# Expert u rows: one load of 1 MB per block, with one semaphore per buffer, in place of two half-row loads

## The reference, cut to what matters

```python
def block(xb):                                   # per block of tokens
    q = (xb @ peer_wq).reshape(PEER_BLOCK, PEER_HEADS, 2, PEER_HALF)
    s = jnp.einsum('thpd,pkd->thpk', q, peer_subkeys).astype(jnp.float32)
    ...                                          # two top-16 lists, their top-16 pairs: eidx, gate
    act = jax.nn.gelu(jnp.einsum('thkd,td->thk', peer_u[eidx], xb))
    return jnp.einsum('thk,thkd->td', gate * act, peer_v[eidx])
```

## Time and profile before

| what | value |
|---|---|
| median of 3 runs | 4359.24 us (4354.56 to 4363.43) |
| the profiled execution | 4361.14 us, its span 4359.4 us |
| TensorE (PE) busy | 4170.0 us, 96% of the span |
| DVE / ACT / POOL busy | 58% / 31% / 16% |
| column phase (blocks 0 to 127) | from about 1840 us to 3233 us |
| value phase | from about 3233 us to 4310 us |

### The profile page before, as it was taken

How to read it: one execution, slowest core, us unless ns; L and a number is a source line. 1 busy time by engine, 2 the same in 40 slices (tenths; PEclk the granted TensorE clock), 3 DMA queues, 4 the chain that set the end, 5 groups by cost and what they waited for, 6 DMA issues and landing times.

```text
span 4359.4 us, 70474 instructions
## 1 busy us (share of the span) xinstructions
PE 4170.0 (96%) x26539; PEld 4004.9 (92%) x26539; DVE 2535.9 (58%) x4045; ACT 1345.8 (31%) x1865; POOL 717.2 (16%) x513
## 2 busy tenths in 40 slices
PE   8998979989899989999999999999999999999996
PEld 6788979989587979999999999999999999999996
DVE  3323233341212355666477746666679888998986
ACT  3432211231212132232355522222223333333333
POOL 0000010020000020024200011111123333344430
PEclk9989989989968999999999999999999999999998
DMA  6532222223431212233334489999999999999993
GB/s 225 203 99 64 73 65 78 69 65 117 167 142 49 73 54 77 79 115 123 124 127 166 169 304 354 355 351 355 356 325 399 410 401 403 392 399 398 400 392 134
DMA packets 495259, 943.14 MB, mean 216 GB/s; under 512 B 126340, under 2 KB 375872, under 8 KB 443000
## 3 DMA queue, kind: packets, MB, share of 16 engines
q1 hardware_dynamic: 443520, 567.36, 39.0%
q0 software_dynamic: 51616, 374.19, 21.4%
HBM read 866.63 MB, written 73.56 MB: 216 GB/s over the span
## 4 chain that ended last, share of the span: by engine, by line
PE 92%; DVE 3%; DMA 2%; ACT 2%; DVEq 1%; issue 0%; POOL 0%; SPq 0%; ACTq 0%
PE pl L1072 24%; PE pp L196 24%; PE pp L1131 12%; PE pt L1131 6%; PE pl L1131 6%; PE pp L1040 5%; PE pt L1049 2%; PE pp L775 2%; PE pp L991 2%; PE pp L956 1%; PE pp L975 1%; PE pt L775 1%; PE pp L842 1%; PE pl L775 1%; PE pt L948 1%; PE pl L1003 1%
## 5 line engine op out<-in xcount | busy, mean ns | idle before, releaser
L1072 PE MATMUL pl<-h_hi,ut_hi 128*128 128x384 f32 x2048 | 734.7, 359 | 0.6 <-ACT ijt L1384 0.6
L1072 PE MATMUL pl<-h_hi,ut_lo 128*128 128x384 f32 x2048 | 692.3, 338 | 0.0
L1072 PE MATMUL pl<-h_lo,ut_hi 128*128 128x384 f32 x2048 | 691.3, 338 | 0.0
L1704 DVE TENSOR_TENSOR ut_lo<-pp,ut_hi 128x512 fp32r<-128x512 f32 x508 | 350.2, 690 | 483.4 <-ACT ut_hi L1337 480.8
L1337 ACT ACTIVATE ut_hi<-pp 128x512 fp32r<-128x512 f32 x508 | 304.0, 599 | 822.0 <-PE pp L1040 765.6
L211 DVE TENSOR_TENSOR w_lo<-raw,w_hi 128x2048 fp32r<-128x2048 f32 x120 | 274.7, 2290 | 425.1 <-ACT w_hi L206 425.0
L1409 ACT ACTIVATE v_hi<-v_raw 128x1024 fp32r<-128x1024 f32 x256 | 272.0, 1062 | 686.0 <-PE pl L1131 508.1
L1072 PEld LDWEIGHTS pl<-h_lo,ut_hi 128*128 128x128 f32 x2048 | 387.1, 189 | 0.0
L1072 PEld LDWEIGHTS pl<-h_hi,ut_hi 128*128 128x128 f32 x2048 | 386.2, 189 | 0.8 <-ACT ijt L1384 0.8
L1806 DVE TENSOR_TENSOR v_lo<-v_raw,v_hi 128x1024 fp32r<-128x1024 f32 x256 | 313.7, 1226 | 124.9 <-ACT v_hi L1409 121.8
L1072 PEld LDWEIGHTS pl<-h_hi,ut_lo 128*128 128x128 f32 x2048 | 384.7, 188 | 0.0
(11 more groups left out here) (359 smaller groups left out, 8262.8 us busy)
## 6 DMA issues: line engine op xcount, KB each, us to landing
u_raw<-in_peer_u SPq DMA_DIRECT2D x256, 512.0 KB
v_raw<-in_peer_v SPq DMA_DIRECT2D x256, 512.0 KB
p_f<-p_scr SPq DMA_DIRECT2D x256, 192.0 KB
raw<-in_w_in SPq DMA_DIRECT2D x24, 1024.0 KB, 5.6
g_scr<-gs POOLq DMA_DIRECT2D x6, 4096.0 KB, 13.7
raw<-in_w_mk SPq DMA_DIRECT2D x16, 1024.0 KB, 4.9
raw<-in_w_mv SPq DMA_DIRECT2D x16, 1024.0 KB, 4.8
raw<-in_w_out SPq DMA_DIRECT2D x16, 1024.0 KB, 5.8
```

The lines of the kernel that those rows point to most:

```text
L1072: last = mm(pl[:, d, 0:N], w[:, d, k, :], x[:, k, S:S + N], start=(k == 0 and w is ut_hi and x is h_hi), stop=(k == KC - 1 and w is ut_lo))
L1704: tt(ut_lo[:, d, 4 * g:4 * g + 4, :], src.rearrange("p (c i) -> p c i", c=4), ut_hi[:, d, 4 * g:4 * g + 4, :].bitcast(F32), ALU.subtract). ...
```

## The change

The two half-row loads of a block become one load of the whole rows. The four semaphores `u_in[d][h]` become two, `u_in[d]`. TensorE waits once per block, at group 0. The load waits for all four groups of block b (`t_done`), where the first half waited for two. In the steady body it stands where the first half stood, ahead of the two `p_scr` stores.

```diff
-        u_in = [[sem(f"u_in{s}{h}") for h in range(2)] for s in range(2)]
+        u_in = [sem(f"u_in{s}") for s in range(2)]
...
-            def u_load(i, d, h, free=None):
+            def u_load(i, d, free=None):
                 if free is not None:
                     sp.wait_ge(t_done, free)
-                sp.dma_start(u_raw[:, d, h * HD:(h + 1) * HD], uv[i * 2 + d][:, h * HD:(h + 1) * HD])\
-                    .then_inc(u_in[d][h], 16)
-            def next_u(i, d, h):
-                u_load(i + 1, d, h, i * 8 + (4 * d + 2 * (h + 1)))
+                sp.dma_start(u_raw[:, d, :], uv[i * 2 + d]).then_inc(u_in[d], 16)
+            def next_u(i, d):
+                u_load(i + 1, d, i * 8 + (4 * d + 4))
...
             def ahead_body(i, d):
-                for h in range(2):
-                    next_u(i, d, h)
+                next_u(i, d)
                 s_store(i + (d - 1), 1 - d)
...
             def steady_body(i, d, first=False):
                 b = i * 2 + d if isinstance(i, int) else None
                 if b is None or b + 2 < NK:
-                    next_u(i, d, 0)
+                    next_u(i, d)
...
                     p_store(i - 1, d)
-                if b is None or b + 2 < NK:
-                    next_u(i, d, 1)
                 g_load(i, d)
...
             def turn_rows(i, d, g, dst, first=False):
-                if g % 2 == 0:
-                    pe.wait_ge(u_in[d][g // 2], i * 16 + 16)
+                if g == 0:
+                    pe.wait_ge(u_in[d], i * 16 + 16)
```

More of the change, by code:

```diff
@@ L664, in _ @@
                 sp.wait_ge(lo_ready, NPANEL - 1 + d)
-                for h in range(2):
-                    u_load(0, d, h)
+                u_load(0, d)
             for d in range(2):
-                for h in range(2):
-                    next_u(0, d, h)
+                next_u(0, d)
                 if d == 1:
```

## The result

| kernel | median us | runs | ratio to before, 95% interval |
|---|---|---|---|
| before | 4359.73 (4354.56 to 4363.43) | 4 | |
| after | 4406.85 (4397.19 to 4410.68) | 4 | 1.0106 [1.0086, 1.0125] |

The change makes the kernel 47 us slower, 1.1%. The prediction was 4359 us, no change, with a range of 4351 to 4374 us; it is wrong. What came is its rival A.

What follows compares the result with a forecast made beforehand. TensorE was taken to pace the column phase, its second half beside nearly full DMA engines. Three parts of 0 each on the profiled 4361.14 us, given as the median: 4359 us, no change (83%), range 4351 to 4374 us.

Steps and rivals of the forecast that it cites:

- rival A: SP's steady body outlasts a column because sa's store lands late behind the full load: 31 us slower, 4390 us; chance 12%.
- Part 1: Removing 128 load issues on SP and 128 TensorE waits before group 2: taken as 0, at most 1.3 us faster.
- rival B: Loads of u_raw: one exposed fixed cost saved per block, up to 384 us; what remains is 3 us; chance 5%.
- Part 2: The u_raw load starts later and is needed earlier by TensorE: taken as 0, upper end 12 us, one time.
- cover of 12.7 us: Time from issuing the full load to group 0 of block b+2 reading it, 5 quarter columns later.
- one late load: In the steady part, seven gathers back to back after the gates' last store could delay a load by 12 us, once.
- Part 3: SP's reordered queue puts sa's store behind the full load; landing taken as T + 7.5 us, so the slip is 0.
- T: The moment the load of block b+2 is issued on SP, just after group 3 of block b is turned.
- bodies with two gathers included: Steady bodies of SP: a second gather, issued 2.8 us after the first, finds sa's store done, so slip 0.
- What waits behind SP: DVE's multiplies and ACT's gelu after the delayed sa, ga, gt loads and fg store: all hidden, costing nothing.
- the slack: In the steady part, a load may be 4.2 us late before group 0 waits; 4 us was taken off the price.
- the dip after T: DMA engines half idle 2.9 us after T (share 0.51), so the full load mostly passes before the first gather's bytes.

Runs made afterwards that it cites:

- e1: The after kernel with its full load issued behind both p_scr stores instead of ahead of them: 4359.06 us, 0.9999 of before.
- e4: The after kernel, same order, with four buffers for sa instead of two and SP's steady loop unrolled: 4360.69 us, 0.9998 of before.
- e8: The after kernel with only the store of sa moved ahead of the full load, the fg store staying behind it: 4360.38 us, 1.0002 of before.
- e7: The before kernel with both half loads issued after group 3 and ahead of the stores, plus four buffers for sa: 4361.03 us, 1.0004 of before.
- e5: The after kernel with POOL's 1 MB gathers of peer_u replaced by 8 KB loads: 4352.36 us, one run.
- run 47: Not a run label: in "the whole run 47" the number is the 47 us by which the after kernel is slower than before.
- e11: The after kernel with its load behind both p_scr stores and one extra tiny DMA issued per steady body behind the load: 4361.35 us, 0.9999 of before.
- e9: The after kernel with row halves 8 KB apart in SBUF, so its single load moves in 4 KB pieces: 4446.21 us, 1.0195 of before.
- e6: The after kernel with its load written as two runs of a row whose halves lie side by side: 4404.83 us, 1.0110 of before.

## Why the prediction was wrong

**Bound and question.** Right: TensorE paces the phase, and no gain was there.

**Part 1.** Taken at 0 to 1.3 us. e1, e4 and e8 have one load and one semaphore and stand at 0.9998 to 1.0002 of before, with the phase at 1393.5 to 1393.6 us: 0 holds. With it falls rival B. (Its 2.0 us are stated in the Trainium skill, DMA: Bandwidth & Descriptors, "Anatomy of one DMA", for the path of DMAs that GpSimd issues, while these are SP's; as nobody waits for the load, no run here shows what a load's fixed cost is worth.)

**Part 2.** The load was taken to land after 5.8 us with free engines, up to 8.5 us beside one gather. It takes 6.8 us in e1 and 7.8 us in after, and the cover of 12.7 us hides it: 0 holds (e1, e4, e7, e8). The "one late load" of up to 12 us didn't come in any of them. In after the transposes do wait for it, since it is issued late and not since it takes long.

**Part 3: the failed step.** The mechanism was set out in full, with its threshold: the store must land by T + 8.6 us. The failed term is its landing. I worked out T + 6.7 to T + 9.4 us and took T + 7.5 us, "since the second half load was through in 3 us at that very place". With SP at its pace it is T + 9.4 us (e4), the upper end of my own interval, 0.8 us past the threshold; in after itself `sa` goes out at T + 9.5 us on average (0.94 + 8.54). Without gathers the store lands at T + 6.2 us (0.6 + 5.6, e5), so the lower end of T + 6.7 us was 0.5 us too high, and the gathers add 3.2 to 3.4 us. That is more than the bytes of one gather (2.6 us): the half-idle windows described the old order, in which the first half had already gone out. In e4 the first gather of a body is issued 1.26 us behind the whole load (2688.23 for 2686.97), and in after, once SP is late, in many bodies ahead of it; the prediction let a gather's bytes begin only at T + 4 us, when most of the load has passed. And a middle value was no fit choice: the answer changes inside the interval, so the interval had to enter the chances as it stood. Some 70% of it, 1.9 of 2.7 us, lay under the threshold, and I gave the rest 12%.

The slip was 0 with "bodies with two gathers included", since the second "finds the store done". That looked for the danger in the wrong place. The body of 2698.77 in after has two gathers behind its load and `sa` out at T + 8.3 us, within the threshold. The loss comes from the bodies whose load stands behind a gather, with `sa` out at T + 10.4 us on average for T + 8.5 us in the others; the prediction doesn't have them. Nor do the two kinds cancel: in that stretch a short body wins back 0.4 us where a long one loses 1.5.

**What waits behind SP.** I had `sa` and `ga` due at T + 16.4 us. One semaphore covers `gt`, `sa` and `ga`, so that all are due at the first product, T + 14.4 us: DVE waited 105.9 us for `ga` in after. In e4, with the same order and no slip, it waited 1.7 us, so this is no cause of its own. A late `fg` store harmless: right (e8).

**Rival A.** Right in mechanism, low in price and chance. Its mean body was 10.8 us, measured 10.87; this nearness is partly luck, since the mean is of two kinds of body, of which it knew nothing. It took off 4 us for the slack and said 31 us; the phase lost 43.1 us, and the whole run 47. Its argument "against", the dip after T, rested on the old order and didn't carry over.

**The value phase.** 8.0 us of after's profiled execution lie behind the last transpose. That stretch took 1121 to 1134 us over all kernels here, 1131.8 us in e11, which isn't slowed. I can't tell it from scatter; not settled.

## What to carry to other kernels

Before moving or merging a load, look at what the same queue waits for afterwards: nobody may be in a hurry to read a small store behind a megabyte, but if the queue's own sequencer waits for it, the whole body becomes load, landing and issues in series, and it only has to be 0.7 us longer than the pace to lose that in each iteration. Put the store whose landing is awaited ahead of the big load, or give its tile more buffers (four for two here); either took back all 47 us, and neither version beats the kernel before. And where a threshold lies inside an estimate's interval, the interval is the result, not its middle.

## What the runs showed of the hardware

- The same 192 KB store took from 5.6 to 9.0 us to its landing: 5.6 us behind a megabyte without gathers (e5), 9.0 us with them (e4), 6.7 us ahead of the load with them (e8).
- An issue isn't a fixed 0.33 us: 588 ns in the middle for the load in 4 KB pieces (e9), and in after 9 of 48 issues of the same load took 0.87 to 2.76 us, each of them 1.6 to 3.5 us behind the issue of a gather. No row of the waits shows this.
- What a load and the store behind it take depends on which was issued first, load or gather: in after the next load came 11.95 us later on average where a gather had been issued up to 3.5 us ahead of the load, 9.72 us later where none had.
- The DMA share fell, 1.00 to 0.94, while the kernel became slower: the mark here of a late issuer and not of full DMA engines.
- Two runs of a row that lie side by side in memory and in the partition were merged into the same 476827 packets (e6).
